# Attention blocks of an encoder layer: the turns of the probabilities before the products with the values, eight places for them, and ScalarE's copies set between its exponentials

## What is computed

```python
def hybrid_mixer(h, ...):
    qa, ka, va, qb, kb, vb, qc, kc, vc = split(h @ w_in)
    oa = neighbourhood_attention(qa, ka, va, rpb)     # "a": 4 heads
    ob = banded_attention(qb, kb, vb, sink)           # "b": 6 query heads, 2 kv heads, window +-128
    oc = dilated_attention(qc, kc, vc)                # "c": 6 heads, 3 branches (dilation 1, 4, 16)
    y = concat([rms_norm(oa), rms_norm(ob), rms_norm(oc)])
    return y @ w_out
# each head, each block of 128 queries: p = exp(score + bias - max); o = (p @ v) / sum(p)
```

## Time and profile before

| | |
|---|---|
| median of three runs | 2332.53 us (2332.25 to 2333.1) |
| the profiled execution | 2333.02 us, its span 2331.3 us |
| mean granted TensorE clock | 0.998 |
| TensorE busy | 2280.3 us, 98% of the span |
| VectorE busy | 1617.7 us, 69% |
| ScalarE busy | 1056.9 us, 45% |
| GpSimd busy | 662.2 us, 28% |
| steps of the eight blocks | about 310 to 435 us in the first layer, 1469 to 1595 us in the second |

### The profile page before, as it was taken

One profiled execution on the slowest core, in us unless ns is written; L12 is line 12 of the kernel. 1 busy time (PEld: TensorE's weight loads), 2 busy tenths in 40 slices (PEclk: granted clock), 3 DMA queues, 4 the chain that ended last, 5 costly groups with the idle time before them and its releaser, 6 DMA issues. The chain is left out here.

```text
span 2331.3 us, 40658 instructions
## 1 busy us (share of the span) xinstructions
PE 2280.3 (98%) x15508; PEld 1885.0 (81%) x15508; DVE 1617.7 (69%) x2921; ACT 1056.9 (45%) x2022; POOL 662.2 (28%) x571
## 2 busy tenths in 40 slices
PE   9999999999999999999999999999999999999999
PEld 9988776787888888888898887667878888888887
DVE  5389989748555555789844999896475555557898
ACT  4333689645222222443533337895452222224434
POOL 1000466312444444100010005562124444440000
PEclk9999999999999999999999999999999999999999
DMA  7231341332222211821352213313322222218223
GB/s 248 65 54 54 82 132 33 124 109 73 82 82 82 82 55 55 313 66 68 118 176 58 55 45 107 107 39 121 104 73 82 82 83 88 60 42 316 69 81 104
DMA packets 234285, 225.35 MB, mean 97 GB/s; under 512 B 50548, under 2 KB 192372, under 8 KB 234104
## 3 DMA queue, kind: packets, MB, share of 16 engines
q1 hardware_dynamic: 234104, 222.90, 30.2%
HBM read 171.00 MB, written 53.41 MB: 96 GB/s over the span
## 5 line engine op out<-in xcount | busy, mean ns | idle before, releaser
L1962 DVE TENSOR_TENSOR WL<-RAW,WH 128x512 fp32r<-128x512 f32 x132 | 160.4, 1216 | 151.4 <-ACT WH L1396 151.4
L2718 PE MATMUL psum<-ABH 128*128 128x512 f32 x616 | 240.1, 390 | 1.1 <-DVE X L2045 1.1
L2720 PE MATMUL psum<-ABH,ABL 128*128 128x512 f32 x616 | 239.7, 389 | 0.0
L2719 PE MATMUL psum<-ABL,ABH 128*128 128x512 f32 x616 | 239.7, 389 | 0.0
L2684 PE MATMUL psum<-HL,WH 128*128 128x512 f32 x704 | 217.4, 390 | 0.7 <-DVE HL L1968 0.7
L2684 PE MATMUL psum<-OPH_t,WH 128*128 128x512 f32 x528 | 206.0, 390 | 3.5 <-DVE U L1983 3.5
L2684 PE MATMUL psum<-OPL_t,WH 128*128 128x512 f32 x528 | 205.7, 390 | 1.0 <-DVE OPH_t L1968 1.0
L1962 DVE TENSOR_TENSOR WL<-WS,WH 128x512 fp32r<-128x512 f32 x172 | 138.4, 806 | 84.2 <-ACT WH L1396 84.2
L2316 POOL TENSOR_TENSOR WS<-RAW 128x512 f32<-128x512 f32 x84 | 143.3, 1706 | 132.0 <-DMA x_res<-X 132.0
L2348 PE MATMUL psum<-HH,UH 128*128 128x512 f32 x448 | 174.5, 389 | 0.0
L2350 PE MATMUL psum<-HH,UL 128*128 128x512 f32 x448 | 174.4, 389 | 0.0
(11 more groups left out here) (276 smaller groups left out, 5546.7 us busy)
## 6 DMA issues: line engine op xcount, KB each, us to landing
RAW<-in_w_gu SPq DMA_DIRECT2D x176, 256.0 KB, 3.9
WDS<-in_w_down SPq DMA_DIRECT2D x88, 256.0 KB, 2.6
UR<-in_w_in SPq DMA_DIRECT2D x56, 256.0 KB, 3.4
g_mid<-GRES SPq DMA_DIRECT2D x28, 512.0 KB, 2.6
WDK<-in_w_down SPq DMA_DIRECT2D x44, 256.0 KB, 6.3
x_res<-X SPq DMA_DIRECT2D x2, 4096.0 KB, 13.4
PR<-in_w_out SPq DMA_DIRECT2D x32, 256.0 KB, 5.1
X<-x_res SPq DMA_DIRECT2D x2, 4096.0 KB, 13.5
```

The source lines that it names most:

```text
L1962: v.tensor_tensor(WL[SLOT[i, j]][:, :, :], w_source(i, j), WH[SLOT[i, j]][:, :, :].bitcast(F32), ALU.subtract).then_inc(w_lo, 1)
L2718: t.matmul(dst, ah, bh, start=open_, stop=False, skip_group_check=True)
L2719: t.matmul(dst, ah, bl, start=False, stop=False, skip_group_check=True)
L2720: last = t.matmul(dst, al, bh, start=False, stop=shut, skip_group_check=True)
```

## The change

For the steps after the dilated ones (`k > DILATED_STEPS`):

- TensorE's order becomes scores, turns, products. In the steps with Y to turn (third and fourth of a block, from the second block on) only T0 goes ahead of P; T1 and Y stay behind it.
- `PT` gets eight places, since the turns of a step are now copied while the places of the step before have not been read. The places come to lie over tables of the dilated steps, which are over by then.
- ScalarE's copies move forward. In steps without Y: e0, copy, e1, copy, e2, copy, e3, and then the store of the group. In steps with Y: e0, copy of group 0, e1, e2, store, copies of group 1 and Y, e3.

VectorE's and GpSimd's orders are as before. No instruction is added or left out, and no wait of one is changed.

```diff
-        PT = sb("PT", [P, 4, 512], F32, "U", 0)
+        PT = sb("PT", [P, 8, 512], F32, "U", 0)
+            def pt_slots(k):
+                return 8 if k > DILATED_STEPS else 4
+                if k == DILATED_STEPS + 1:
+                    n_pt = 4
...
-                        if j == 2:
-                            for n in weighed_at(k):
-                                if family_end(n):
-                                    store_result(n)
-                            for u in mine[:1]:
-                                copy_unit(u)
-                    for u in mine[1:]:
-                        copy_unit(u)
+                        if k <= DILATED_STEPS:
+                            if j == 2:
+                                store_results(k)
+                                for u in mine[:1]:
+                                    copy_unit(u)
+                        elif any(u["y"] for u in mine):
+                            if j == 0:
+                                copy_unit(mine[0])
+                            elif j == 2:
+                                store_results(k)
+                                for u in mine[1:]:
+                                    copy_unit(u)
+                        elif mine[j:j + 1]:
+                            copy_unit(mine[j])
+                    if k <= DILATED_STEPS:
+                        for u in mine[1:]:
+                            copy_unit(u)
+                    elif not any(u["y"] for u in mine):
+                        store_results(k)
...
+                    if k <= DILATED_STEPS:
+                        products(k)
+                        turn_units(k, range(len(steps[k])))
+                    else:
+                        finished = any(u["y"] for u in steps[k])
+                        ahead = [i for i, u in enumerate(steps[k]) if not (finished and u["group"])]
+                        turn_units(k, ahead)
+                        products(k)
+                        turn_units(k, [i for i in range(len(steps[k])) if i not in ahead])
```

More of the change, by code:

```diff
@@ L129, in build_program @@
         PL = sb("PL", [P, 4, 512], F32R, "R")
-        PT = sb("PT", [P, 4, 512], F32, "U", 0)
+        PT = sb("PT", [P, 8, 512], F32, "U", 0)
+        at["U"] = place["U"]
         UR = sb("UR", [P, 2, KD, P], F32, "U")
@@ L542, in build_program @@
                             for half in range(2):
-                                rows.append(dict(y=None, items=[], engine=None, bank=pair_[half], slot=n_pt % 4, half=half,
+                                rows.append(dict(y=None, items=[], engine=None, bank=pair_[half], slot=n_pt % pt_slots(k), half=half,
                                                  group=group, pair=pair_))
@@ L1291, in tail_scale, with store_results @@
                                  scale=grstd[:, i:i + 1]).then_inc(y_s[i], 1)
+                def store_results(k):
+                    for n in weighed_at(k):
+                        if family_end(n):
+                            store_result(n)
                 def act_step(k):
@@ L2564, in pe_step, with products @@
                         pe.wait_ge(rmsq_s, 2 * QT - 1)
+                    if k <= DILATED_STEPS:
[7 more added lines that the diff above has]
+                        turn_units(k, [i for i in range(len(steps[k])) if i not in ahead])
+                def products(k):
                     for n in weighed_at(k):
@@ L2568, in pe_step, with turn_units @@
                         weigh(n)
-                    for i, u in enumerate(steps[k]):
+                def turn_units(k, which):
+                    for i in which:
+                        u = steps[k][i]
                         if k in (1, 3):
```

## The result

The changed kernel takes 2346.99 us, the median of four runs (2346.79 to 2348.89), where four runs of the kernel before took 2332.82 (2332.25 to 2334.22). The ratio is 1.0058, 95% interval 1.0046 to 1.007: 14 us slower. The last experiments' record holds 27 executions of the kernel before with a median of 2334.24 (2330.24 to 2337.03); against that it is 12.8 us slower. The forecast was 2340.5 with 2346 as the upper end of its range. The direction was right, the size was too small by 6 us (5 by the larger sample), and the time lies 1 us outside the range.

What follows compares the result with a forecast made beforehand. TensorE is busy nearly throughout, but VectorE sets the pace in a block's first half and at the fourth step's S2. 4.25 plus 0.5 less 0.75 is 4.0 us a layer, 8 in both: 2340.5 us, range 2329 to 2346.

Steps and rivals of the forecast that it cites:

- Second step, T1 waits for m1: Middle block's second step: group 1 turns wait 1.17 us for VectorE's second pass, products queued behind; signs 0.6 to 1.2 us.
- The middle term: Middle blocks: each costs 0.85 us more, between 0.6 and 1.1; five in each layer make 4.25 us.
- the lower bound: Middle block: the coefficient takes 0.16 us, not 0.69, and the block costs 0.6 us more.
- The lower cost of 0.6: Middle block: a short coefficient brings the second step's first two passes up to 0.5 us sooner, so cost is 0.6 us.
- my upper bound: Middle block: about 1.1 us more if VectorE's work between stays as long.
- First step, wait of 0.15 us: Middle block's first step: group 1 turns wait about 0.15 us for VectorE's second pass, VectorE working on undisturbed.
- The waits before S2: Middle block: fourth step's 0.32 us wait for VectorE's copy stays; third step's for ScalarE's copy goes, winning nothing.
- The eight places: Places of PT: they only let copies be early and add no work; priced at nothing.
- ScalarE's order: ScalarE's later last exponential and store: priced at nothing; up to 0.5 us a block if the cover were gone.
- The edges: First and last blocks of a layer: 0.5 us lost at the start, 0.75 gained at the last block.
- much slower: ScalarE falls behind too: Rival: late last exponential or store costs each middle block another 0.5 us, 6 in all; 2346 to 2348, chance 0.1.

Runs made afterwards that it cites:

- x4: The changed kernel with VectorE's squares of branch b in a second step moved behind its third pass and the mean behind its fourth; 2341.37 us, ratio 1.003.
- z1: y1 with ScalarE's copy of group 0 ahead of the stores of finished groups in every step; 2331.74 us, ratio 0.9991.
- z4: The kernel before with only the eight places of PT added, all orders as before; 2334.28 us, ratio 1.0.
- x2: The changed kernel with ScalarE's old order put back, TensorE's new order and the eight places kept; 2351.58 us, ratio 1.007.
- y4: The changed kernel with all exponentials ahead of ScalarE's copies of Y in the last steps (k = 54 on); 2347.81 us, ratio 1.006.
- y1: The kernel before with VectorE's squares of group c moved behind its copy of group 0's turn in a block's third step; 2329.34 us, ratio 0.9977.
- z3: The changed kernel with both engines' old orders at k = 25 and from k = 53 on, so changed in the middle only; 2344.65 us, ratio 1.0048.
- x3: The changed kernel with only group 0 turns ahead of the products in all steps, and ScalarE's copies reordered to suit; 2339.94 us, ratio 1.0028.
- z2: z1 with the coefficient of branch b behind VectorE's copy of the first step; 2331.24 us, ratio 0.9987.
- x1: The changed kernel with TensorE's old order put back, ScalarE's new order and the eight places kept; 2357.82 us, ratio 1.0101.

## Why the prediction was right in direction and too small

- **Second step, T1 waits for m1.** Right in kind and place: 22 waits for VectorE's pass at the turns, the longest 1.1 us, and 0.89 in the second step of a middle block, within the 0.6 to 1.2 foretold. x4, which moved m1, moved the block.
- **The middle term**, 0.85 us a block: measured 0.90 on the mean of ten, in the forecast's bounds. That it came so near is in part luck, since its make-up was not as I had it. The coefficient did come out at 0.16 us, as the lower bound had it: GpSimd began at 359.80, 0.08 us behind it, where before it began 0.18 ahead of it. The Trainium skill, GPSIMD Engine Reference, section Specifications, has the two engines contend for shared SBUF interfaces; the 0.69 and 0.16 us agree with that, and it names no size. The lower cost of 0.6 that I had tied to the short coefficient did not come with it: the 0.5 us so won did not reach m1, since m0 of the second step then waited 0.35 us for its scores. The first step had become 0.35 longer (3.84 from S1 to S1, not 3.49), and the second 0.73 (4.68, not 3.95). In the clean block that makes 1.11 us, my upper bound; over the other blocks, which take 15.74 to 16.59 us before and 16.69 to 17.16 after, it makes 0.57 to 0.95, and the mean is 0.90.
- **First step, wait of 0.15 us**: it was 0.36. T1 starts 0.66 behind the start of m1, not 0.59, and T0 was done 1.88 us after S1, not 2.0. I also let VectorE work on undisturbed there, and its 0.35 us wait shows that it didn't.
- **The waits before S2**: 0.32 in the fourth step stayed and the third step's went, as foretold, and as foretold this won nothing (z1 shows the same in the old kernel).
- **The eight places** at nothing: z4 shows it. **ScalarE's order** at nothing: true of the middle blocks beside TensorE's order, which needs it (x2), not at the edges, where the late store makes VectorE wait at the start.
- **The step that failed is "The edges".** It put 0.5 us on the start of a layer's blocks and a gain of 0.75 on the last block, -0.5 us in both layers together. The runs show a loss at both edges. In the one pair of profiles it is 3.75 us: 1.91 and 0.26 at the start, 1.65 and -0.07 at the end. The means of profiles with the same orders are steadier. At the start the kernel before and z4 take 19.25 us, the changed kernel and y4 20.33: 1.1 us a layer, of which k = 29 alone is 0.9. I had put its T1 at 3.26 us behind S1 and T1 with the products at 1.43; they took 3.43 and 1.60, and I then took 0.5 for the 0.6 of my own sum. The late store, which I had looked for nowhere but in the middle, comes on top in the first layer. The last block gained nothing: the order costs about 0.6 us where I had 0.75 won. The waits that I expected to go did go, but T0 waits for a copy of Y (0.51 us), Y for GpSimd (1.19), and the last turns 1.34 us for e3, which the prediction followed only in a middle step.
- **What is left.** By the pair of profiles the edges are 4.25 of the 6.5 us by which the forecast was short, the middle term another 0.5, and no changed order that I know of explains the remaining 1.75. Against the larger sample of the kernel before the forecast was short by only 4.8 us, so most of those 1.75 can be the small first sample. Both profiles have a stretch of low granted clock in the second layer's end, and the changed kernel alone in the first's: some 1.4 us of the pair's edges, and not shown to be the change's.
- **The rivals.** The time came out where "much slower: ScalarE falls behind too" had put it, 2346 to 2348, but not by its mechanism: in a middle block no turn waits for e3. That rival did see that e3 and the store were what a full ScalarE would make late; it looked for them in the wrong blocks.

## What to carry to other kernels

Work that is moved ahead needs what it reads and the place that it writes; list both, and what now sits behind it in its queue, before the move is taken for free: here the turns could go early only where VectorE's pass and ScalarE's copies of the step before were over, and each experiment that freed one side found the other. Walk the first and the last repetition of a pattern as carefully as the middle one, with their stores and transfers: ten middle blocks were forecast to 0.05 us each, in part by luck, and the edges missed by 4 us. And where a wait is to be shortened, look for what stands ahead of its releaser in that engine's queue and is needed by nobody soon: moving one such operation (y1) gained 0.23%, and the reordering of two engines lost 0.58%.

## What the runs showed of the hardware

TensorE's granted clock falls to about half for some 4 us at the end of this stage in some executions and layers and not in others, with the same orders and the same waits ahead of it (z3: one layer of two). It costs about 1.4 us each time, and so can account for much of the spread between runs of one kernel: the runs of y1 with a mean granted clock of 1.0 took 2325.91 and 2326.74 us, those with 0.998 took 2329.43 and 2330.43.

One of the ten executions of x3 took 3765.51 us at a mean granted clock of 0.556, where the other nine took 2338.15 to 2342.38 us at 0.998 to 1.000.

An operation of 128x6 elements on VectorE takes 0.16 us when it begins 0.08 us ahead of GpSimd's operation and 0.69 when it begins 0.18 behind. z2 has more such starts:

```profile
421.53 0.84 POOL L2278 TENSOR_TENSOR G<-G,fac_c 128x390 f32<-128x390 f32 x1 [3.44 <-ACT fac_c L1254]
421.93 0.46 DVE L1753 TENSOR_TENSOR coef<-den,fac_b 128x6 f32<-128x6 f32 x1
```

| begins behind GpSimd's operation by | takes | ends behind GpSimd's start by |
|---|---|---|
| 0.03 (x1) | 0.82 | 0.86 |
| 0.18 (before) | 0.69 | 0.86 |
| 0.40 (z2) | 0.46 | 0.86 |
| 0.64 (z2) | 0.22 | 0.86 |
| 0.70 (z2) | 0.16 | 0.86 |

GpSimd's operation takes 0.84 us each time. So the small operation on VectorE, once begun behind GpSimd's, does not end before that one is over, however early in it it began. It goes both ways. The 128x384 operation behind the coefficient takes 0.55 us when it begins with no operation of GpSimd under way, 0.80 when it begins 0.45 us into one (the kernel before) and 1.15 when it begins 0.10 into one (z2); in both of these it ends 0.41 us behind the end of GpSimd's operation. And GpSimd's next operation, which it then overlaps, takes 1.15 us where the others take 0.84, and ends 0.70 behind the end of VectorE's in both.
